# Reordering the gated delta section and moving masks, decays and gatings from GpSimd to VectorE

## What is computed

```python
u = rmsnorm_2(h, mix_norm) @ w_mix_in
cb, cc, ch, gq, gk, gv, gz, gb, ga = split(u)
y_conv = group_rmsnorm(cb * causal_depthwise_conv(cc * ch, conv_short_w))        # short convolution, 3 taps
q, k, v = split(silu(causal_depthwise_conv(concat(gq, gk, gv), gdn_conv_w)))     # 4 taps
q, k = l2norm(q), l2norm(k)
beta, g = sigmoid(gb), -exp(A_log) * softplus(ga + dt_bias)                      # then cumsum of g within a chunk
lower = where(strict, (k*beta) @ k.T * decay, 0)                                 # decay = exp(g_i - g_j)
u, w = solve((I + lower), [v*beta, k*beta*exp(g)])                               # unit lower triangular
attn = where(causal, q @ k.T * decay, 0)
# over the chunks: v_new = u - w @ state; o = (q*exp(g)) @ state + attn @ v_new
#                  state = state * exp(g_last) + (k*exp(g_last - g)).T @ v_new
y_gdn = rmsnorm_2(o, norm_w) * silu(z)
h = h + concat(y_conv, y_gdn) @ w_mix_out
```

## Time and profile before

| | us |
|---|---|
| median of 3 runs | 2346.67 |
| lowest, highest | 2342.52, 2346.86 |
| the profiled execution | 2346.58 |
| its span | 2344.7 |
| its mean granted TensorE clock | 0.986 of full speed |
| TensorE busy in it | 2277.3 (97%) |
| delta section, from its first matmul to the end of its last piece | 1589.80 to 1945.2 |

### The profile page before, as it was taken

The page is one execution under the profiler, slowest core; times in us unless marked ns, Lnnn a source line. Parts: engine busy times, 40 slices in busy tenths (PEclk is TensorE's granted clock), DMA queues, the critical chain, the costliest instruction groups (busy, mean ns, idle before and its releaser), DMA issues.

```text
span 2344.7 us, 27218 instructions
## 1 busy us (share of the span) xinstructions
PE 2277.3 (97%) x10322; PEld 1873.4 (80%) x10322; DVE 1057.2 (45%) x1066; ACT 739.4 (32%) x973; POOL 694.9 (30%) x482
## 2 busy tenths in 40 slices
PE   8999999999999999999999999998898999999997
PEld 6888888788777888888887888885797777888885
DVE  5444334444546454434445434335635445444323
ACT  4222223232233242222333222223553224222221
POOL 3444104500222014444114444301361013444300
PEclk9999999999999999999999999999899899999998
DMA  4333334333222323332332333332101122333332
GB/s 141 97 98 98 99 108 126 96 111 99 66 71 80 96 93 99 98 94 94 108 107 90 98 96 92 107 107 65 45 2 54 54 73 92 96 98 98 99 106 82
DMA packets 58817, 213.16 MB, mean 91 GB/s; under 512 B 6529, under 2 KB 6785, under 8 KB 58625
## 3 DMA queue, kind: packets, MB, share of 16 engines
q1 hardware_dynamic: 58464, 210.02, 28.4%
q0 software_dynamic: 288, 2.23, 0.3%
HBM read 210.13 MB, written 2.10 MB: 91 GB/s over the span
## 4 chain that ended last, share of the span: by engine, by line
PE 91%; issue 3%; DMA 2%; DVE 2%; POOL 2%; ACT 1%; POOLq 0%; SPq 0%; DVEq 0%; ACTq 0%
PE acc L485 28%; PE acc L487 28%; PE acc L486 28%; DMA w_raw<-weights 2%; PE mixb L933 1%; PE acc L876 1%; PE acc L875 1%; PE acc L877 1%; PE sums L515 1%; PE mixb L748 1%; POOL r_raw L1920 0%; PE mixb L913 0%; PE acc L758 0%; PE mixb L758 0%; POOL qk L1928 0%
## 5 line engine op out<-in xcount | busy, mean ns | idle before, releaser
L485 PE MATMUL acc<-x_hi,w_hi 128*128 128x512 f32 x2016 | 801.0, 397 | 11.1 <-DVE x_lo L1345 9.6
L486 PE MATMUL acc<-x_lo,w_hi 128*128 128x512 f32 x2016 | 789.4, 392 | 0.0
L487 PE MATMUL acc<-x_hi,w_lo 128*128 128x512 f32 x2016 | 789.4, 392 | 0.0
L485 PEld LDWEIGHTS acc<-x_hi,w_hi 128*128 128x128 f32 x2016 | 382.2, 190 | 94.9 <-DVE x_lo L1345 10.1
L1326 DVE TENSOR_TENSOR w_lo<-w_raw,w_hi 128x1024 fp32r<-128x1024 f32 x232 | 304.9, 1320 | 325.9 <-ACT w_hi L984 325.1
L486 PEld LDWEIGHTS acc<-x_lo,w_hi 128*128 128x128 f32 x2016 | 382.1, 190 | 80.2 <-issue 2.4
L487 PEld LDWEIGHTS acc<-x_hi,w_lo 128*128 128x128 f32 x2016 | 381.3, 189 | 80.7
L984 ACT ACTIVATE w_hi<-w_raw 128x1024 fp32r<-128x1024 f32 x232 | 243.1, 1054 | 394.2 <-DMA w_raw<-weights 394.2
L1384 DVE TENSOR_TENSOR w_lo<-w_raw,w_hi 128x1024 fp32r<-128x1024 f32 x160 | 245.1, 1532 | 271.1 <-ACT w_hi L990 271.1
L485 PE MATMUL acc<-hid_hi,w_hi 128*128 128x512 f32 x704 | 273.9, 389 | 0.0
L486 PE MATMUL acc<-hid_lo,w_hi 128*128 128x512 f32 x704 | 273.9, 389 | 0.0
(11 more groups left out here) (331 smaller groups left out, 1949.0 us busy)
## 6 DMA issues: line engine op xcount, KB each, us to landing
w_raw<-weights SPq DMA_DIRECT2D x392, 512.0 KB, 3.5
h<-x_t SPq DMA_DIRECT2D x4, 512.0 KB, 6.4
y_t<-h SPq DMA_DIRECT2D x8, 256.0 KB, 2.2
k1c<-const POOLq DMA_DIRECT2D x1, 1536.0 KB, 7.7
k2c<-const POOLq DMA_DIRECT2D x1, 641.0 KB, 5.5
cst<-const SPq DMA_DIRECT2D x1, 161.0 KB, 8.2
vec<-vectors SPq DMA_DIRECT2D x1, 112.5 KB, 2.1
```

Source lines behind the costliest of these rows:

```text
L485: pe.matmul(bank, w_hi[:, slot, w], hi, start=start, stop=False)
L486: pe.matmul(bank, w_hi[:, slot, w], lo, start=False, stop=False)
L487: return pe.matmul(bank, w_lo[:, slot, w], hi, start=False, stop=stop)
```

## The change

- The five tables are new: the same jobs on other engines, and in another order on every engine. The order of the 28 + 4 weight blocks stays.
- `lv`, `el` and `ea` on GpSimd are gone. `first` multiplies the unmasked `lower_t`, and the mask is applied when VectorE evacuates the product (`pm`, in place of ScalarE's `pc`). `ld` applies beta, the norms and the decay at once while it evacuates, as four instructions for four heads. The causal mask is applied when the transposed scores are evacuated (`at`, now on VectorE). The first level (`yi`) becomes two instructions in place of GpSimd's one and VectorE's one.
- `cg` and `cp` are gone from GpSimd: the evacuation of an h block multiplies by the c block, which was scaled by the square of the norm (`nsq`, `rstd2`); the evacuation of a b block multiplies by the convolution.
- The state's decay moves from GpSimd into `st` on VectorE, four instructions for four heads.
- The first tap of each convolution moves from VectorE to ScalarE (`tp`, 12 times, and `ctp`, 4 times).
- The mean of the short convolution's norm is made on VectorE (`cmean`); ScalarE then takes only the root.
- `turnk` transposes three chunks in place of four.

```diff
 ACT_ORDER = _jobs("""
-    w w abc w nroot troot w sg w sqk0 kc0 sg sqk1 kc1 sg w sqk2 kc2 sg sqk3 abx w sg w rk sqq0 cumx kc3 sg
 ...
+    w w abc nroot troot tp w sg tp abx w tp sg w sqk0 cumx sg tp w sqk1 sqk2 exp0 exp1 sg kc0 kc1 exp2 tp w
 ...
-                for t in range(NT):
+                for t in range(NT - 1):
 ...
                 bank = take(("first", (c, i)), p_copied[c], k)
-                pe.wait_ge(m_ready[c], k + 1)
+                pe.wait_ge(lt_copied, c + 1)
                 pe.wait_ge(x_copied[c], k)
                 for hd in range(HEADS):
-                    last = pe.matmul(bank[:, hd * P:(hd + 1) * P], chunk(level_mp, c)[:, hd, :],
+                    last = pe.matmul(bank[:, hd * P:(hd + 1) * P], chunk(lower_t, c)[:, hd, :],
                                      chunk(lower_x, c)[:, hd, :], start=True, stop=True)
                 last.then_inc(p_done[c], 1)
 ...
-
-            def p_copy(c, i):
-                act.wait_ge(p_done[c], i + 1)
-                act.activation(chunk(level_mp, c), bank_of("first", c, i), ACT.Copy).then_inc(p_copied[c], 1)
 ...
+            def first_tap(ci):
+
+                name = CONV[ci]
+                act.wait_ge(drained, a + BLOCKS.index(name) + 1)
+                if ci >= 2:
+                    act.wait_ge(silu_done, SILU_OF[CONV[ci - 2]] + 1)
+                act.activation(c_acc[:, ci % 2, :], c_raw[:, ci % 2, 1:1 + S], ACT.Copy,
+                               scale=vcol("gdn_conv_w_2", HEADS * "qkv".index(name[0]) + int(name[1]))).then_inc(tap_done, 1)
 ...
                 name = BLOCKS[j]
                 kind, i, u = name[0], int(name[1]), int(name[1]) % 2
                 dve.wait_ge(block_done, n + j + 1)
-                bank = acc[j % 2][:, :]
+                bank, scale = acc[j % 2][:, :], rstd[:, :]
                 if kind in "kqv":
-                    out = c_raw[:, CONV.index(name) % 2, 4:]
+                    ci = CONV.index(name)
+                    if ci >= 2:
+                        dve.wait_ge(conv_done, ci - 1)
+                    out = c_raw[:, ci % 2, 4:]
                 elif kind == "z":
                     out = z_t[:, i, :]
+                elif kind == "c":
+                    dve.wait_ge(ab_done, 2)
+                    out, scale = c_gate[:, u, :], rstd2[:, :]
                 elif kind == "h":
+                    dve.wait_ge(drained, a + BLOCKS.index(f"c{i}") + 1)
+                    dve.wait_ge(conv_done, len(CONV))
+                    if i >= 2:
+                        dve.wait_ge(c_conv, i - 1)
+                    out, scale = c_raw[:, u, 4:], c_gate[:, u, :]
+                else:
+                    dve.wait_ge(c_conv, i + 1)
                     dve.wait_ge(v_turned, HEADS)
                     if i >= 2:
+                        dve.wait_ge(c_hi, i - 1)
                         dve.wait_ge(c_split, i - 1)
-                    out = c_y[:, u, :]
-                else:
-                    if kind == "c":
-                        dve.wait_ge(ab_done, 2)
-                        if i >= 2:
-                            dve.wait_ge(c_prod, i - 1)
-                    else:
-                        dve.wait_ge(c_gated, i + 1)
-                    out = c_gate[:, u, :]
-                dve.tensor_tensor(out, bank, rstd[:, :], ALU.mult).then_inc(drained, 1)
+                    out, scale = c_y[:, u, :], c_acc[:, u, :]
+                dve.tensor_tensor(out, bank, scale, ALU.mult).then_inc(drained, 1)
 ...
             def lower(c):
+
                 dve.wait_ge(kk_done, c + 1)
-                dve.wait_ge(el_done, c + 1)
-                dve.tensor_tensor(chunk(lower_x, c), bank_of("kk", c), chunk(lower_x, c), ALU.mult).then_inc(l_done, 1)
+                dve.wait_ge(exp_done, c + 1)
+                dve.wait_ge(k_scaled, 1)
+                bank = bank_of("kk", c)
+                for hd in range(HEADS):
+                    last = dve.scalar_tensor_tensor(chunk(lower_x, c)[:, hd, :], bank[:, hd, :],
+                                                    sm("beta_n2")[:, 4 * c + hd:4 * c + hd + 1],
+                                                    chunk(decay_a, c)[:, hd, :], ALU.mult, ALU.mult)
+                last.then_inc(l_done, 1)
 
             def scores(c):
                 dve.wait_ge(qk_done, c + 1)
-                dve.wait_ge(ea_done, c + 1)
+                dve.wait_ge(l_done, c + 1)
                 dve.tensor_tensor(chunk(decay_a, c), bank_of("qk", c), chunk(decay_a, c), ALU.mult).then_inc(a_done, 1)
 
+            def scores_turned(c):
+
+                dve.wait_ge(a_turned, c + 1)
+                dve.tensor_tensor(chunk(decay_a, c), bank_of("turna", c), over_heads(C_TRI), ALU.mult).then_inc(at_copied, 1)
 ...
             def first_inverse(c):
 
-                dve.wait_ge(m_ready[c], 1)
-                dve.tensor_tensor(chunk(y_inv_t, c), ident_h, chunk(level_mp, c), ALU.subtract).then_inc(y_step[c], 1)
+                dve.wait_ge(lt_copied, c + 1)
+                step(dve.tensor_tensor(chunk(y_inv_t, c), chunk(lower_t, c), over_heads(C_LEVEL), ALU.mult))
+                dve.tensor_tensor(chunk(y_inv_t, c), chunk(y_inv_t, c), ident_h, ALU.add).then_inc(y_step[c], 1)
+
+            def level(c, i):
+
+                dve.wait_ge(p_done[c], i + 1)
+                dve.tensor_tensor(chunk(level_mp, c), bank_of("first", c, i), over_heads(C_LEVEL + (i + 1) * P),
+                                  ALU.mult).then_inc(p_copied[c], 1)
 
 ...
-                    dve.wait_ge(state_scaled, c)
-                    dve.tensor_tensor(state, state, bank_of("su", c), ALU.add).then_inc(state_done, 1)
+                    dve.wait_ge(qs_done, c)
+                    bank = bank_of("su", c)
+                    for hd in range(HEADS):
+                        last = dve.scalar_tensor_tensor(state[:, hd, :], state[:, hd, :],
+                                                        sm("e_total")[:, 4 * c + hd:4 * c + hd + 1], bank[:, hd, :],
+                                                        ALU.mult, ALU.add)
+                    last.then_inc(state_done, 1)
 
 ...
-                pool.tensor_tensor(c_raw[:, u, 4:], c_y[:, u, :], c_gate[:, u, :], ALU.mult).then_inc(c_gated, 1)
-
-            def conv_product(i):
-                u = i % 2
-                pool.wait_ge(drained, a + BLOCKS.index(f"b{i}") + 1)
-                pool.wait_ge(c_conv, i + 1)
-                pool.tensor_tensor(c_y[:, u, :], c_acc[:, u, :], c_gate[:, u, :], ALU.mult).then_inc(c_prod, 1)
```

More of the change, by code:

```diff
@@ L402, in build @@
         at_copied = sem("at_copied")
-        m_ready = [sem(f"m_ready{i}") for i in range(NT)]
         p_done = [sem(f"p_done{i}") for i in range(NT)]
@@ L1651, in taps @@
+                dve.tensor_tensor(out, bank, scale, ALU.mult).then_inc(drained, 1)
             def taps(ci):
                 name, u = CONV[ci], ci % 2
-                kind, hd = name[0], int(name[1])
-                dve.wait_ge(drained, a + BLOCKS.index(name) + 1)
-                if ci >= 2:
-                    dve.wait_ge(silu_done, SILU_OF[CONV[ci - 2]] + 1)
-                channel = HEADS * "qkv".index(kind) + hd
-                for tap in range(4):
+                channel = HEADS * "qkv".index(name[0]) + int(name[1])
@@ L1660, in taps @@
+                dve.wait_ge(tap_done, ci + 1)
+                for tap in range(1, 4):
                     w = vcol("gdn_conv_w_2", 12 * tap + channel)
                     src = c_raw[:, u, 1 + tap:1 + tap + S]
-                    if tap == 0:
-                        step(dve.tensor_scalar(c_acc[:, u, :], src, w, None, ALU.mult))
-                    else:
-                        ins = dve.scalar_tensor_tensor(c_acc[:, u, :], src, w, c_acc[:, u, :], ALU.mult, ALU.add)
-                        if tap == 3:
-                            ins.then_inc(conv_done, 1)
-                        else:
-                            step(ins)
+                    ins = dve.scalar_tensor_tensor(c_acc[:, u, :], src, w, c_acc[:, u, :], ALU.mult, ALU.add)
+                    if tap == 3:
+                        ins.then_inc(conv_done, 1)
+                    else:
+                        step(ins)
@@ L1772, in conv_taps, with conv_mean @@
                 u = i % 2
-                dve.wait_ge(c_gated, i + 1)
-                dve.wait_ge(silu_done, max(ALL_OF[kind] for kind in "kqv"))
-                if i >= 2:
-                    dve.wait_ge(c_prod, i - 1)
-                for tap in range(3):
+                dve.wait_ge(c_tap_done, i + 1)
+                for tap in (1, 2):
                     w = vcol("conv_short_w_2", 4 * tap + i)
                     src = c_raw[:, u, 2 + tap:2 + tap + S]
-                    if tap == 0:
-                        step(dve.tensor_scalar(c_acc[:, u, :], src, w, None, ALU.mult))
-                    else:
-                        ins = dve.scalar_tensor_tensor(c_acc[:, u, :], src, w, c_acc[:, u, :], ALU.mult, ALU.add)
-                        if tap == 1:
```

(16 more changed lines are left out.)

147 lines of the change are left out of this document (62 added, 85 removed), and 6 rows, old and new, of the table BANKS.

## The result

The changed kernel takes 2278.26 us (median of four runs, 2277.11 to 2279.37). The kernel before takes 2344.77 us over the runs beside it. The ratio is 0.9722, with a 95% interval of 0.9704 to 0.974. The forecast was 2289.0, in a range of 2281 to 2315. The sign and the mechanism were right.

What follows compares the result with a forecast made beforehand. PE was taken to bound the kernel, losing 64.1 us in the delta section to waits and lowered clock. 2346.6 - 34.4 (idle) - 23.1 (clock) - 0.4 (transposes) = 2288.7, forecast 2289.0 us, range 2281 to 2315.

Steps and rivals of the forecast that it cites:

- What bounds the kernel, and the views: Whole kernel: PE is busy for 97% of the span, and its busy share dips only around the 355.4 us delta section.
- 64.1 us ... is the most that a new order can win.: Delta section: 38.4 us of PE idle time plus 25.7 us of lost clock cap the gain; PE's own work stays.
- One cause: Delta section: ScalarE's weight splits, queued before their transfers landed, hold up roots and squares PE needs; 38.4 us idle.
- The other 7 us are short waits of the same kind: Delta section: PE's idle time outside the six main wait kinds was put down to the same cause, 7 us.
- Term 1: PE's idle time in the delta section: falls from 38.4 to 4 us, gain 34.4 us (26.4 to 38.0).
- the sum for late splits: Weight splits in the delta section: 10.2 us are free before PE needs a block, and none moved by more than 5.
- Term 2: PE's clock in the delta section: dips go with the gaps, gain 23.1 us (12.9 to 25.7) of 25.7.
- No drop came without a gap: PE's clock in the delta section: each of the ten low stretches follows a gap of PE.
- Term 3: Work moved between engines in the delta section: hidden behind PE, costed at nothing; four transposes fewer give 0.4 us.
- threshold for a masked evacuation: Rounds of the levels: VectorE's work stays hidden until one masked evacuation costs more than 1.4 us.
- The rivals: Half of 64.1 us stays, 2314.5, 17%; clock stays low, 2311.8, 7%; order does nothing, 2346, 3%; slower, 2361, 3%.
- half stays: Convolution blocks: ScalarE and VectorE chains run late, so half of 64.1 us stays, 2314.5 us; chance 17%.

Runs made afterwards that it cites:

- e5_order_more: The kernel before with only order changed: ScalarE's and VectorE's weight splits later, block 13's split behind the last level's copies, merges right after each output half; 2297.72 us.
- e4_square_5: The changed kernel with the squares of convolution groups 1 to 3 made six times instead of once; 2285.38 us.

## Why the prediction was right, and where it was not

- **What bounds the kernel, and the views.** Right: the difference lies in the section, 67.1 us, with 1.4 us in the stretch ahead of it and 0.5 behind. The section began between 1588.3 and 1589.8 in all profiles, whatever the kernel, so the 1.4 us are the spread of the start.
- **"64.1 us ... is the most that a new order can win."** This step failed: it took PE's busy time, but for the clock, as work that an order cannot touch. The section gave 67.1 us. The idle column gave its 38.4 us exactly. Of PE's busy time 317.0 - 288.3 = 28.7 us went: 24.8 of clock (I had 25.7), 0.4 for the four transposes, and 3.5 us that are neither. A matmul of a dense block is shown with 0.39 us from start to end, at a pace of 0.227, so the last one ahead of any wait is counted busy for 0.16 us in which the stream would have gone on. For the 20 waits of 0.1 us and more in the section of the kernel before that makes 3.2 us. The repeated squares test it where no dip disturbs: three waits brought 0.70 us of busy time, where 0.16 each makes 0.5. How much of the 3.5 us hangs on the number of waits stays open all the same: the three order variants of before have 15 or 16 such waits, 2.5 us by this count, and still 3.5 us. The Trainium skill, TensorE: Matmul & The Clock Gate, section "Step-by-step: what each phase is for", tells the same of the matmul: "The 128-cycle drain of one matmul overlaps the 128-cycle fill of the next". The two figures, 0.39 and 0.227, agree with it in that matmuls overlap; since the ends in the trace are modelled, they do not measure the drain.
- **One cause.** Half right. "The other 7 us are short waits of the same kind" was a misreading: 3.3 of them named GpSimd's products (`turnk` 2.2, `turnv` 1.1) and 3.0 the merges, none of them a split that waited for its transfer. Moving ScalarE's splits alone gave 21 us of 66. VectorE's splits gave 17 more, two more changes of order 7, and the rest came with the new tables as a whole. The prediction read the chain of waits, which names only the last link; the other input of the square came 0.44 us earlier. For `csum` its sum nevertheless came out right, since it dropped GpSimd's product and split with one stroke.
- **Term 1.** The hand-made plan left 0.4 us, and the trace shows 0.0. The 4 us that I kept for the scatter of hand-offs did not come. No wait for weights (`w_lo`) appeared either, as the sum for late splits had it.
- **Term 2.** The dips went with the gaps, all ten; the 2.6 us kept for one dip were not needed. "No drop came without a gap" held in every variant, though in e5_order_more a gap of 0.91 us was the only one near its second drop.
- **Term 3.** The masked evacuations cost 0.69 us each, as taken, and the four-part forms 4 x 0.34 = 1.4 us where I took 1.1 within 0.7 to 2.8:

```profile
L1732 DVE TENSOR_TENSOR level_mp<-mixb,k2c 128x512 f32<-128x512 f32 x12 | 8.3, 690 | 4.2 <-PE mixb L744 4.2
L1766 DVE SCALAR_TENSOR_TENSOR sumsq<-sumsq,small,mixb 128x128 f32<-128x128 f32 x8 | 2.2, 341 | 3.1 <-PE mixb L795 3.1
```

  Hidden, as said. The prediction's threshold for a masked evacuation, 1.4 us, was too high, since it added up VectorE's work and left out the chain: at 1.4 us per mask the kernel had already lost 5.9 us.
- **The rivals.** None came. Against "half stays" the prediction put 145 us for twelve convolution blocks; the trace shows no wait at all there.
- **The miss, added up.** 11.2 us too little: 4.0 kept for waits, 2.6 kept for a dip, 3.5 not counted less 0.9 counted too much, 1.9 outside of the section, 0.1 of rounding. Both kept sums were put in against the prediction's own plan. The lower end kept only 0.4 us of waits and no dip, 2282.5, and the profiled execution lies 5.0 us below it too: 0.4 of waits, 2.6 of PE's busy time, 1.9 outside of the section and rounding. So the cap of 64.1 us is the largest term that the range had no room for; the 1.9 us, the scatter of the start among them, are chance and no merit of the change.

## What to carry to other kernels

In an in-order queue, put nothing that waits for a transfer ahead of something another engine waits for; look for the same mistake on every engine of the chain, and ask for each wait when the second-latest input came, since the last link alone is worth only the distance to it. Test an order before rewriting the work: here order alone, tried by hand in two tables, gave 47 of 67.1 us, and four kinds of moved work together 2.3 us. When the waits of the busiest engine go, count the clock dips and the end of the last matmul ahead of each wait with them. And where the new order has been walked through with measured durations, a reserve needs a row that supports it; here none came, in one case.

## What the runs showed of the hardware

- Gaps of PE of 4.4 to 4.6 us cost 3.0 us each more in clock. Gaps of 1.8 to 1.9 us cost no dip in one kernel (e4_square_5) and one in another (before, at 1894.34), and in the kernel before 2.25 us passed without one where 2.19 did not.
- A wait of PE costs about 0.2 us beyond the idle time that the profile shows: 0.70 us for three waits, of which 0.16 each is the overlap that the last matmul's shown end hides.
- GpSimd working beside VectorE (73.9 us against 28.5 us in the section) cost no more than 2.3 us, although in the kernel before the three taps of one convolution took 3.88 us beside two GpSimd products and 2.33 us without any:

```profile
1613.94 2.33 DVE L1665 SCALAR_TENSOR_TENSOR c_acc<-c_raw,vec,c_acc 128x512 f32<-128x512 f32 x3
...
1684.29 3.88 DVE L1665 SCALAR_TENSOR_TENSOR c_acc<-c_raw,vec,c_acc 128x512 f32<-128x512 f32 x3
```

  The Trainium skill, SBUF — State Buffer, section "SBUF: two separate sides", says that GpSimd and a VectorE instruction with two inputs in SBUF, as a tap has, take turns on a port pair they share, one of them blocked for a whole instruction. The longer taps agree with it; the time of the kernel hardly notices; VectorE is busy for only 186 of the section's 291 us in that run.
